# Two reorderings at the end of the gated linear attention layers of a four-layer decode step

## The reference, cut to what matters

```python
q, k, v, g, a = split(rmsnorm(x) @ w_in)
logf = log_sigmoid(a @ w_a2 + b_a) / 16
# per head: S_t = diag(exp(logf_t)) S_{t-1} + k_t^T v_t ;  o_t = q_t S_t
x = x + (rmsnorm(o, g_on) * silu(g)) @ w_out
```

## Time and profile before

| what | us |
|---|---|
| median of 3 runs | 1209.37 (1208.86 to 1212.71) |
| the profiled execution: its time | 1208.89 |
| the profiled execution: span from first to last instruction | 1207.1 |
| PE busy in it | 1162.4 |
| granted TensorE clock, mean over the span | 0.996 |

### The profile page before, as it was taken

How to read it: one execution, slowest core, us unless ns; L and a number is a source line. 1 busy time by engine, 2 the same in 40 slices (tenths; PEclk the granted TensorE clock), 3 DMA queues, 4 the chain that set the end, 5 groups by cost and what they waited for, 6 DMA issues and landing times. The chain is left out here.

```text
span 1207.1 us, 25033 instructions
## 1 busy us (share of the span) xinstructions
PE 1162.4 (96%) x9937; PEld 1026.0 (85%) x9937; DVE 601.3 (50%) x1183; ACT 557.9 (46%) x1088; POOL 381.8 (32%) x322
## 2 busy tenths in 40 slices
PE   8999999999999999999999989999999999999897
PEld 6889887898678998888965549999999889988797
DVE  6462355756079999010015544589266253245652
ACT  6542466544324355444544444432454344266643
POOL 5544131245313511122200013534445254411330
PEclk9999999999999999999999999999999999999999
DMA  5235235133505256767669882232321136234212
GB/s 183 76 113 162 75 115 183 45 84 93 182 1 178 71 182 213 237 232 218 221 236 409 334 312 87 72 104 71 124 77 38 36 105 192 71 105 158 88 36 74
DMA packets 127788, 168.78 MB, mean 140 GB/s; under 512 B 20384, under 2 KB 93480, under 8 KB 127663
## 3 DMA queue, kind: packets, MB, share of 16 engines
q1 hardware_dynamic: 115609, 152.59, 38.8%
q10 hardware_dynamic: 12062, 14.59, 3.4%
HBM read 150.70 MB, written 16.81 MB: 139 GB/s over the span
## 5 line engine op out<-in xcount | busy, mean ns | idle before, releaser
L671 POOL TENSOR_TENSOR w_lo<-raw,w_hi 128x512 fp32r<-128x512 f32 (+2 forms) x267 | 359.9, 1379 | 729.5 <-ACT w_hi L1425 729.5
L707 PE MATMUL psum<-h_hi,w_hi 128*128 128x272 f32 x1616 | 471.6, 292 | 6.0 <-DVE h_lo L2343 4.7
L709 PE MATMUL psum<-h_hi,w_lo 128*128 128x272 f32 x1616 | 467.2, 289 | 0.0
L708 PE MATMUL psum<-h_lo,w_hi 128*128 128x272 f32 x1616 | 464.8, 288 | 0.0
L707 PEld LDWEIGHTS psum<-h_hi,w_hi 128*128 128x128 f32 x1616 | 303.4, 188 | 16.8 <-issue 12.3
L708 PEld LDWEIGHTS psum<-h_lo,w_hi 128*128 128x128 f32 x1616 | 303.7, 188 | 0.1
L709 PEld LDWEIGHTS psum<-h_hi,w_lo 128*128 128x128 f32 x1616 | 302.9, 187 | 0.0
L1425 ACT ACTIVATE w_hi<-raw 128x1024 fp32r<-128x1024 f32 (+1 forms) x137 | 135.5, 1035 | 114.5 <-PE psum L709 79.5
L707 PE MATMUL psum<-w_hi,h_hi 128*128 128x512 f32 (+2 forms) x352 | 124.6, 354 | 0.0
L709 PE MATMUL psum<-w_hi,h_lo 128*128 128x512 f32 (+2 forms) x352 | 121.0, 344 | 0.0
L708 PE MATMUL psum<-w_lo,h_hi 128*128 128x512 f32 (+2 forms) x352 | 120.9, 343 | 0.0
(11 more groups left out here) (327 smaller groups left out, 1493.6 us busy)
## 6 DMA issues: line engine op xcount, KB each, us to landing
raw<-in_cache_k_dram SPq DMA_DIRECT2D x128, 256.0 KB, 3.1
raw<-in_gla_w_in_dram SPq DMA_DIRECT2D x23, 1024.0 KB, 5.4
spare<-in_cache_v_dram SPq DMA_DIRECT2D x36, 512.0 KB, 6.4
raw<-in_dsa_w_in_dram SPq DMA_DIRECT2D x17, 1024.0 KB, 6.4
raw<-in_cache_v_dram SPq DMA_DIRECT2D x28, 512.0 KB, 6.0
gla_s_in<-in_state_gla_dram SPq DMA_DIRECT2D x16, 512.0 KB, 7.9
raw<-in_gla_w_out_dram SPq DMA_DIRECT2D x8, 1024.0 KB, 6.9
out_dram<-gla_s_in ACTq DMA_DIRECT2D x16, 512.0 KB, 4.1
```

Of the source, the lines that this page charges most:

```text
L671: pool.tensor_tensor(copies(key, pair_view(w_lo, key)[:, k]), raw_copies(key, k), copies(key, pair_view(w_hi, key)[:, k].bitcast(F32)), AL ...
L707: pe.matmul(out, lh, rh, start=start, stop=False)
L708: pe.matmul(out, lh, rl, start=False, stop=False)
L709: return pe.matmul(out, ll, rh, start=False, stop=stop)
```

## The change

The load of state 7 is issued behind output item 2 with states 5 and 6, so ahead of output item 3. And the second output item is rounded in one go, both halves behind `branch_hi(5)`; before, the first half stood between `branch_hi(3)` and `branch_hi(4)`. Both are in both GLA layers. No instruction is added or removed and no size changes.

```diff
-                    for b in {(L, "g", 0): (0, 1, 2), (L, "out", 1): (3, 4), (L, "out", 2): (5, 6),
-                              (L, "out", 3): (7,)}.get(key, ()):
+                    for b in {(L, "g", 0): (0, 1, 2), (L, "out", 1): (3, 4), (L, "out", 2): (5, 6, 7)}.get(key, ()):
                         state_load(L, b)
...
                 branch_hi(2)
                 branch_hi(3)
-                split_hi(pair_of[(L, "out", 1)], (0,))
                 branch_hi(4)
                 branch_hi(5)
-                split_hi(pair_of[(L, "out", 1)], (1,))
+                split_hi(pair_of[(L, "out", 1)])
                 act.preload_act_table_set(EXP_LN)
```

## The result

The changed kernel took 1212.99 us (median of 20 runs, 1207.51 to 1220.74) against 1208.76 us of the kernel before (20 runs, 1205.55 to 1213.83). The ratio is 1.0034 [1.0023, 1.0045], so the change costs 4.1 us, between 2.8 and 5.4. The forecast was 1212.3. The execution shown here took 1210.62 us for a span of 1208.8 us. In the changed kernel the lines behind the diff stand one or two lower: L1069 is now L1068, L950 is L949, L707 is L706, `root` (four instructions, L2262 and L2264 to L2266) is L2260 and L2262 to L2264, L2275 is L2273 and L2343 is L2341.

A forecast was written before the change was run, and what follows sets the result against it. PE, busy for 96% of the span, was taken as the bound, so only its waits could be won. -2.0 (state load) + 2.8 (rounding) + 2.4 (clock) = +3.2 us gave 1212.3 us, range 1207.0 to 1214.0.

The forecast's parts named there:

- State 7, -2.0 us: PE's waits for decode state 7 in both GLA layers go: 1.15 us gained in layer 3, 0.86 in layer 0.
- Rounding, +2.8 us: Before the `last_rows` transposes in both GLA layers, POOL's pieces delay DVE's normalising; transposes 1.4 us later per layer, +2.8 us.
- The rival without hindrance: DVE and POOL don't hinder each other before the last transposes; rounding costs 0, total -2.0 us, 1207.1; chance 0.12.
- the one in which all is gained: No stall before `last_rows`; both PE waits go in each GLA layer, 4.8 us gained, 1204.3; chance 0.05.
- The clock, +2.4 us: PE's longer stall before the last transposes lowers the granted clock, 1.6 us each time, chance 3 in 4 per GLA layer.
- the sign that the prediction gave for being wrong: Clock staying at 1.00 across a 2.8 us wait before the last transposes would show the prediction wrong.
- the chance of 3 in 4: Chance, in each GLA layer, that the clock falls at the stall before the last transposes, costing 1.6 us.
- within 0.3%: Whole kernel's time stays within 3.6 us, about what a measurement can tell from none; chance 0.66.
- slower: Whole kernel slower by over 0.3%: the worse case, or the clock falling fully twice; chance 0.29.

The follow-up runs named there:

- the kernel with one wait: Kernel before with state 7's load moved and POOL holding all four pieces of the second output item until `low(5)` is done: 1208.96 us, ratio 1.0007.
- the short pieces: Changed kernel with POOL subtracting only 8 of each 256 columns of the second output item in the GLA layers: 1206.70 us, ratio 0.9991.
- the stall is filled: Changed kernel with 18 unread products on PE before the last transposes: 1210.39 us, ratio 1.0031; run again, 1209.46 us, ratio 1.0010.
- the kernel before with short pieces: Kernel before, POOL subtracting only 8 of each 256 columns of the second output item in both GLA layers: 1206.39 us, ratio 0.9994.

## Why the prediction held, step by step

**The measure for the steps.** Where the clock plays no part, the distance on PE from its readiness for sequence 7 to the last transposes sums up both edits. Before it was 18.24 us in layer 0 and 18.52 in layer 3 (226.41 less 208.17, 1149.73 less 1131.21). In the changed kernel it is 18.85 and 18.84 us, with state 7 alone 17.52 and 17.51. So the two edits together cost 0.61 + 0.32 = 0.9 us of waiting, where the prediction had -2.0 + 2.8 = +0.8.

**State 7, -2.0 us.** The mechanism is shown: issued at about 1112, no wait at L1068, and the transposes of pieces 0 and 1 held 0.2 us by tile 3. The distance gained 0.72 + 1.01 = 1.7 us and the full-clock time 1.3 ± 0.4. The term was somewhat too large: of the waits of 0.96 and 1.26 us the wait for tile 3 left 0.24 and 0.25, where the prediction had 0.10 and 0.11. It also rests on one execution's waits, and in layer 0 that was 0.96 us in the execution of the earlier trace rows, but 0.55 and 0.64 in two others with the same load order. The verdict of this half alone is 1.0000; its gain is only seen once the clock, which was lower in those runs (6.6 against 5.3 us, a difference of 1.4 ± 0.8) though its profiled execution shows 1.00 at the ends of both layers, is taken out. Why it was lower is open.

**Rounding, +2.8 us.** From state 7 alone to both edits the distance grows by 1.33 us in each layer, 2.7 us in all, and the rounding alone measured +2.4 ± 0.4 at full clock. Inside the term: `low(5)` at 0.7 us and PE without a wait there, as said; POOL's pieces 5.03 us (5.1 said); L2260 1.09 and L2262 1.20 us (1.1 and 1.2 said), each ending with a piece; the stall 2.6 us (2.85 said, 0.2 less, about as much as the distances fell short). That POOL is the cause for 1.53 of the 2.61 us is shown by making its pieces short, and from the other side by the kernel with one wait, where ACT is early and the stall is there. The rival without hindrance is refuted by the same rows, and the one in which all is gained with it. Its price was about right, though: with the short pieces the transposes come 0.2 us earlier per layer than with state 7 alone, where that rival had 0.

The Trainium skill, "GPSIMD Engine Reference", section Specifications, has GpSimd and VectorE contend for their shared SBUF interfaces when the VectorE instruction has two SBUF inputs or a two-port mode. The trace agrees for L2262, with 1.20 against 0.17 us. L2260 has one tensor input and was held too (1.09 against 0.17 us); which of the two clauses covers it no run here shows.

**The clock, +2.4 us.** Measured as clock loss beyond that of the kernel before: +2.5 us with the rounding alone, +2.1 and +1.9 with both edits, none or 0.9 once the stall is filled. These means alone would not settle it, as two kernels without such a stall, state 7 alone and the kernel before with short pieces, stand at +1.4 ± 0.8 and +1.3 ± 0.6. The profiled executions do. Behind the stalls of 2.6 us the clock fell in three of six in the changed kernel and in two of two with the rounding alone, and behind those of 2.2 us in one of two; in the nine other executions, whose waits there are 1.4 us or less, it never fell in the 18 layer ends, the four filled ones among them. So the lower clock comes from PE standing still there, but not each time: the sign that the prediction gave for being wrong, a clock of 1.00 across such a wait, is there in three of eight cases. Five of eight agrees with the chance of 3 in 4, and no more. Each fall took 1.6 to 1.7 us, as said.

**The sum.** +3.2 us was forecast; the three comparisons have +4.1, +4.3 and +2.9 us by the ratios. The 20 runs of the changed kernel lost 8.6 us to the clock at a full-clock time of 1203.8; the clocks of the 20 runs of the kernel before beside them are not on record, so what is above the forecast can't be split. That terms and sum agree so closely is in part luck: the stalls were a little shorter than forecast, the gain of state 7 a little smaller, and each set of runs differs from the next by about 1 us. The chances had within 0.3% at 0.66 and slower at 0.29; 0.34% lies on the far side of that bound, by 0.5 us. The forecast of +3.2 us lay only 0.4 us below the bound, so the chance of slower was set too low.

**What stays open:** whether the filling products have a part in the surplus of 1.2 to 1.5 us at full clock, seen twice; why PE's waits for the cache loads of layer 1 differ by 3 us between executions; and the lower clock of the kernels with state 7 alone and with short pieces in the old order.

## What to carry to other kernels

Before taking work out from under one wait, look at the next place where the same engine only just arrives in time: here 0.23 us of slack in the timeline of before told that removing 1.4 us would not come through. A row of POOL instructions, queued and ready, lengthened each dependent short DVE instruction beside it to about POOL's piece length here, as long as pieces were left; making POOL wait for the end of the chain cost PE 0.4 us per layer and brought the chain back. And a gain or loss of a few us in a kernel whose PE is 96% busy should be split into waiting and clock before it is explained: for the rounding alone they were +2.4 and +2.5 us.

## What the runs showed of the hardware

An instruction on five numbers took 0.17 us alone and up to 1.21 us beside POOL, and the sharing goes instruction by instruction: when a held DVE instruction gets through, POOL's next piece goes before the next dependent DVE instruction. It took one such piece for each of up to three chained instructions (1.09 and 1.20 us, or 0.62, 1.21 and 1.21), and DVE's own long instructions lengthened POOL's row from 5.01 to 5.91 us. A stall of 2.6 us did not always have the same consequence for the clock: at one and the same place it read 0.59 over the next 4 us in layer 0 and 1.00 in layer 3, and in another execution of the same kernel the clock fell in layer 3 and not in layer 0. In all it fell behind five of eight such stalls, and behind none of 1.4 us or less at these places.
